# One decoder layer on one core: cached keys worked off inside the attention heads, a filled last head, a new order of the pooling branch, and the samples' projection in 16 matmuls

## What is computed

```python
h = _rms_norm(x, p['g_mix'], RMS_EPS)
z = h @ p['w_in']                      # pool channels u | q | k | v | gate_pool | gate_attn
q = _rope(z[..., OFF_Q:OFF_K]...)
k = _rope(z[..., OFF_K:OFF_V]...)
pool_out = _pool_mixer(u_full, pos, p['w_pool_grp'], p['pool_scale'])
# 4 groups of 128 channels, windows 2, 4, 8, 16: window mean - token, group matmul, scale
# prompt: causal attention; samples: over the cached keys and values and their own
s = jnp.einsum('bqhcd,bkhcd->bhcqk', q, k) * (HEAD_DIM ** -0.5)
p = jax.nn.softmax(s, axis=-1)
a = p[:, :, 0] - lam * p[:, :, 1]
o = jnp.einsum('bhqk,bkhe->bqhe', a, v)
merged = (gate_pool * (pool_out @ p['w_pool_proj'])
          + gate_attn * (o.reshape(B, T, D_ATTN) @ p['w_attn_proj']))
x = x + merged @ p['w_o']
x = x + jnp.square(jax.nn.relu(_rms_norm(x, p['g_mlp'], RMS_EPS) @ p['w_up'])) @ p['w_down']
```

## Time and profile before

| | us |
|---|---|
| median of 3 runs | 1842.93 (1841.47 to 1843.98) |
| the profiled execution | 1843.01 |
| its span | 1841.2 |
| TensorE busy | 1772.3 (96%) |
| VectorE busy | 935.5 (51%) |
| ScalarE busy | 544.3 (30%) |
| GpSimd busy | 244.4 (13%) |

### The profile page before, as it was taken

One profiled execution on the slowest core, in us unless ns is written; L12 is line 12 of the kernel. 1 busy time (PEld: TensorE's weight loads), 2 busy tenths in 40 slices (PEclk: granted clock), 3 DMA queues, 4 the chain that ended last, 5 costly groups with the idle time before them and its releaser, 6 DMA issues.

```text
span 1841.2 us, 27590 instructions
## 1 busy us (share of the span) xinstructions
PE 1772.3 (96%) x11428; PEld 1711.4 (93%) x11428; DVE 935.5 (51%) x1404; ACT 544.3 (30%) x1040; POOL 244.4 (13%) x284
## 2 busy tenths in 40 slices
PE   7999999999969699999999999999999999999997
PEld 6899888988959698999999999999999999999997
DVE  5677777777765987672225434421442244224323
ACT  4355545454543212121113332211220122012202
POOL 3211221222102554520000000000000000000001
PEclk9999999999989898999999999999999999999999
DMA  6211220222024474651122221111111111111112
GB/s 191 59 41 30 70 59 12 70 70 58 13 63 146 135 261 155 217 202 57 46 58 78 74 57 46 46 46 47 46 46 47 46 47 57 47 35 46 58 46 93
DMA packets 177988, 139.03 MB, mean 76 GB/s; under 512 B 7232, under 2 KB 163840, under 8 KB 177855
## 3 DMA queue, kind: packets, MB, share of 16 engines
q1 hardware_dynamic: 176711, 133.07, 23.8%
q10 hardware_dynamic: 1152, 4.19, 0.6%
HBM read 120.29 MB, written 17.18 MB: 75 GB/s over the span
## 4 chain that ended last, share of the span: by engine, by line
PE 82%; DVE 9%; issue 4%; ACT 2%; POOL 1%; DMA 1%; SPq 1%; DVEq 0%; ACTq 0%
PE ps L666 60%; PE ps L580 13%; PE ps L635 3%; PE ps L602 2%; PE ps L625 1%; DVE w_lo L1182 1%; DVE mx L1233 1%; POOL o_rstd L1662 1%; DMA w_raw<-in_w_in 1%; DVE win L1368 1%; DVE y_st L1624 1%; PE ps L799 1%; POOL kv_pages L1684 0%; DVE w_lo L1347 0%; DVE o_st L1268 0%
## 5 line engine op out<-in xcount | busy, mean ns | idle before, releaser
L666 PE MATMUL ps<-h_hi,w_hi 128*128 128x344 f32 x1248 | 270.2, 325 | 7.3 <-DVE w_lo L1347 3.8
L666 PE MATMUL ps<-h_lo,w_hi 128*128 128x344 f32 x1248 | 268.2, 324 | 0.0
L666 PE MATMUL ps<-h_hi,w_lo 128*128 128x344 f32 x1248 | 267.0, 323 | 0.0
L1038 ACT ACTIVATE w_hi<-w_raw 128x1024 fp32r<-128x1024 f32 x106 | 111.9, 1055 | 443.7 <-PE ps L666 439.1
L666 PEld LDWEIGHTS ps<-h_hi,w_hi 128*128 128x128 f32 x1248 | 213.5, 192 | 8.1 <-DVE w_lo L1347 4.1
L666 PEld LDWEIGHTS ps<-h_lo,w_hi 128*128 128x128 f32 x1248 | 214.0, 191 | 0.0
L666 PEld LDWEIGHTS ps<-h_hi,w_lo 128*128 128x128 f32 x1248 | 211.4, 191 | 0.0
L580 PE MATMUL ps<-w_hi,h_hi 128*128 128x384 f32 (+1 forms) x576 | 202.1, 351 | 4.2 <-DVE w_lo L1182 3.7
L580 PE MATMUL ps<-w_hi,h_lo 128*128 128x384 f32 (+1 forms) x576 | 195.7, 340 | 0.0
L580 PE MATMUL ps<-w_lo,h_hi 128*128 128x384 f32 (+1 forms) x576 | 194.9, 338 | 0.0
L1347 DVE TENSOR_TENSOR w_lo<-w_raw,w_hi 128x1024 fp32r<-128x1024 f32 x106 | 138.6, 1308 | 81.5 <-ACT w_hi L1038 81.5
(11 more groups left out here) (221 smaller groups left out, 2782.6 us busy)
## 6 DMA issues: line engine op xcount, KB each, us to landing
w_raw<-in_w_in SPq DMA_DIRECT2D x44, 512.0 KB, 5.5
kv_pages<-in_cache_k SPq DMA_DIRECT2D x32, 512.0 KB, 5.1
kv_pages<-in_cache_v SPq DMA_DIRECT2D x32, 512.0 KB, 5.0
w_raw<-in_w_up SPq DMA_DIRECT2D x32, 512.0 KB, 4.0
w_raw<-in_w_down SPq DMA_DIRECT2D x32, 512.0 KB, 3.6
out<-kv_st SPq DMA_DIRECT2D x16, 512.0 KB
x_in<-in_x_prompt SPq DMA_DIRECT2D x8, 512.0 KB, 5.3
attention_out_scratch<-oT_st ACTq DMA_DIRECT2D x8, 512.0 KB, 2.7
```

The lines of the kernel that those rows point to most:

```text
L666: mm = pe.matmul(ps[:, SET[sp] + c, 0:CH], w, a[:, c * CH:(c + 1) * CH], start=(first and m == 0), stop=(last and m == 2))
L1038: act.activation(w_hi[:, lp], w_raw[:, lp], ACT.Copy).then_inc(s_whi, 1)
```

## The change

1. **Samples' projection.** For heads 1 to 7, tile 8 of `project` uses `h_samples`, written once: columns 0 to 7 the high half of the samples' h, columns 8 to 39 four copies of the low half. One matmul of 40 rows with `w_hi` gives high x high in rows 0 to 7 and low x high in rows 32 to 39, one of 8 rows with `w_lo` the third part: 16 matmuls, not 24. ScalarE copies rows 32 to 39 out (`sample_low`), VectorE adds (`z_smp`), and `rotate` reads `z_smp`.
2. **Keys in the heads.** In head `h`, for each sample `b`, SyncE loads only that head's 128 columns of four pages into a ring of four `key_ring` buffers; GpSimd multiplies all four pages with `q_bc` in one instruction of 128x512 (`key_products`, behind `rotated` of the steps in `KEYS_AT`); VectorE sums them at the end of the step behind (`sum_keys`). `kv_st` shrinks to a ring of four tiles, and SyncE stores each tile for itself (`store_tile`).
3. **Last head.** The product `("u", 0)` is cut into 24 units of three matmuls (one chunk of 344 tokens, one of eight input blocks), spread over the steps of head 7 by `FILL`. ScalarE and VectorE split its weights in steps 0 and 3, not ahead of step 0. The samples' own scores (`own_step`) are in steps 3 to 5.
4. **New order behind.** Two buffers `up`, `u 1`, `u 2` and `u 3` with the group products between them, then gates and pooling projections from tile 7 down to 0; the cached values behind the entries of `VALUES_AFTER`.

```diff
-PART_A = [("u", 0), ("u", 1), ("grp", 0), ("u", 2), ("grp", 1), ("u", 3), ("grp", 2), ("gate", 0), ("grp", 3),
-          ("pool", 0), ("gate", 1), ("pool", 1), ("gate", 2), ("pool", 2),
-          ("gate", 3), ("pool", 3)]
-N_A = 4
-REDUCE_AT = (1, 3, 5, 7, 9, 10, 11, 13)
+PART_A = [("u", 0), ("u", 1), ("u", 2), ("grp", 0), ("u", 3), ("grp", 1), ("gate", 7), ("grp", 2), ("gate", 6), ("grp", 3),
+          ("pool", 7), ("pool", 6)]
+KEYS_AT = {2: (0, 1), 3: (2, 3), 4: (4,), 5: (5,), 6: (6,), 7: (7,)}
...
             def project(hp, t, half):
+                if hp and t == NTT:
+                    for kt in range(4 * half, 4 * half + 4):
+                        both = (bank[0:LOW_ROW + DEC, 0:3 * P], h_smp[:, kt], w_hi[:, :, kt, :])
+                        small = (bank[0:DEC, 0:3 * P], h_smp[:, kt, 0:DEC], w_lo[:, :, kt, :])
...
             def rotate(hp, t):
+                if hp and t == NTT:
+                    dve.wait_ge(s_zl, hp)
+                    dve.tensor_tensor(z_smp[0:n], bank[0:n, 0:3 * P], z_smp[0:n], ALU.add).then_inc(s_zs, 1)
+                    dve.wait_ge(s_zs, hp)
+                    bank = z_smp
...
+            def sum_keys(h, b):
+                dve.wait_ge(s_prod, DEC * h + b + 1)
+                dve.tensor_reduce(sc_all[:, :, b * 16 + 2 * h:b * 16 + 2 * h + 2],
+                                  kc[:, key_slot(h, b)].rearrange("p g (c e) -> p g c e", c=2), AX_X,
+                                  ALU.add).then_inc(s_kred, 1)
...
+                    for b in KEYS_AT.get(s - 1, ()):
+                        sum_keys(h, b)
+                    if not proj and s in (0, 3):
+                        low(s // 3)
+                    if not proj and 3 <= s <= 5:
+                        own_step(s - 3)
...
+            def key_products(h, b):
+                slot = key_slot(h, b)
+                pool.wait_ge(s_qb, 16 * (h + 1))
+                pool.wait_ge(s_kc[slot], 16 * PAGES * (key_uses(h, b) + 1))
+                pool.tensor_tensor(kc[:, slot], kc[:, slot], q_bc[:, b].unsqueeze(1).to_broadcast([P, PAGES, P]),
+                                   ALU.mult).then_inc(s_prod, 1)
...
+            for h in range(HEADS - 1):
+                spread_q(h)
+                for s in range(NTT + 1):
+                    store_tile(h + 1, s)
+                    if s == 1 and h < HEADS - 2:
+                        load_qkv(h + 2)
...
+                    keys_behind(h, s)
...
+            def pool_product(n):
+                if n == KT - 1:
+                    tile_out(pe, grp_tile(NG - 1))
+                product(pool_tile(n), y_hi, y_lo, NG)
```

More of the change, by code:

```diff
@@ L699, in head @@
                         project(h + 1, s, 0)
+                    elif s < NTT:
+                        fill(s, 0)
                     if s == NTT:
@@ L705, in head @@
                         weight_transposes(h, s - 1, 1, proj)
+                    if not proj:
+                        fill(s, 1)
                     if normed and s == 3:
@@ L738, in _, with fill @@
             last = HEADS - 1
-            u_tiles = [t for s_, kind, n, t in part_a() if kind == "u"]
+            filled = [0]
+            def fill(s, place):
+                for unit in range(filled[0], filled[0] + FILL.get((s, place), 0)):
+                    c, kt = unit // KT, unit % KT
+                    if unit == 0:
+                        pe.wait_ge(s_zfree, 9 * HEADS)
+                        pe.wait_ge(s_wlo, W_QKV + 1)
+                    elif kt == 0:
+                        pe.wait_ge(s_u0e, c)
+                    cols_ = slice(c * CH, (c + 1) * CH)
+                    for m, (w, a) in enumerate(((w_hi, h_hi), (w_hi, h_lo), (w_lo, h_hi))):
+                        mm = pe.matmul(bank_z[:, 0:CH], w[:, 0, kt], a[:, kt, cols_], start=(kt == 0 and m == 0),
+                                       stop=(kt == KT - 1 and m == 2))
+                    if kt == KT - 1:
+                        mm.then_inc(s_u0 if c < NCH - 1 else s_tile, 1)
+                filled[0] += FILL.get((s, place), 0)
             def first_product(first, behind):
-                product(u_tiles[0], h_hi, h_lo, KT, part=(first, behind))
+                product(u_tile(1), h_hi, h_lo, KT, part=(first, behind))
             head(last, 1, False, True)
             values(last, 1, NTT - 1)
-            first_product(6, KT)
             def last_head_out():
+                pe.wait_ge(s_us, 1)
                 out_transposes(last, 1, 0, (ps[:, 6], ps[:, 7]))
@@ L823, in _, with group @@
-            pe.wait_ge(s_vout, 2)
-            for i in range(0, DEC // 2):
-                product(gate_tile(i), h_hi, h_lo, KT)
-                cached_values(i, 0)
-                product(pool_tile(i), y_hi, y_lo, NG)
-                cached_values(i, 1)
-            for i in range(DEC // 2, KT - N_A):
-                product(gate_tile(i), h_hi, h_lo, KT)
-                product(pool_tile(i), y_hi, y_lo, NG)
+            def group(g):
+                t = grp_tile(g)
+                pe.wait_ge(s_pllo, g + 1)
+                pe.wait_ge(s_wglo, 1)
+                need(pe, s_free[t[1]], t[0])
+                passes(t[1], wg_hi[:, g], wg_lo[:, g], pl_hi, pl_lo, True, True)
@@ new lines, in gate_product @@
+            def gate_product(n, between=None):
+                product(gate_tile(n), h_hi, h_lo, KT, between=between)
+                if ("gate", n) in VALUES_AFTER:
+                    cached_values(VALUES_AFTER["gate", n])
+            def pool_product(n):
+                if n == KT - 1:
+                    tile_out(pe, grp_tile(NG - 1))
+                product(pool_tile(n), y_hi, y_lo, NG)
+                if ("pool", n) in VALUES_AFTER:
+                    cached_values(VALUES_AFTER["pool", n])
@@ L986, in head @@
                         o_out(h - 1, 1 - par, NTT - 1)
+                    if not proj and s in (3, 6, 8):
+                        first_chunk_out(s // 3 - 1 if s < 8 else 2)
                     if s >= 1:
@@ new lines, in _ @@
+            pooled_high(2)
+            gate_high(7)
+            group_high(2)
+            pooled_high(3)
+            gate_high(6)
+            group_high(3)
+            act.wait_ge(s_tail, NG)
+            act.activation(tail_st[0:BUF + DEC], bank_o[0:BUF + DEC, 0:D_POOL], ACT.Copy).then_inc(s_tailc, 1)
+            next_high(pool_tile(7))
+            next_high(pool_tile(6))
+            for n in range(KT - N_A - 1, -1, -1):
+                gate_high(n)
+                next_high(pool_tile(n))
```

665 lines of the change are left out of this document (365 added, 300 removed).

## The result

The changed kernel takes **1854.75 us** (median of 5 runs, 1851.27 to 1856.55) against 1842.95 for the kernel before in the same session (5 runs, 1841.47 to 1843.98): ratio 1.006, 95% interval 1.0045 to 1.0075. It is 0.6% slower; forecast were 1824 us, with 1800 to 1843 as the range. The profiled execution has a span of 1853.9 us, where before it was 1841.2: 12.7 us more.

What follows compares the result with a forecast made beforehand. It took TensorE as full in middle heads, with VectorE and ScalarE's loop nearly as long, and chains as the bound in the last head; 1843.0 + 12.6 + 3.7 + 9 - 44 = 1824 us, range 1800 to 1843.

Steps and rivals of the forecast that it cites:

- What bounds a middle head: Middle heads: TensorE is full, but VectorE and ScalarE run a loop nearly as long; slack at `bank_z` 1.4 us.
- Rival A: Heads stay TensorE's: slack absorbs the sums and 1.4 us a head are won; 1798 us, chance 0.13.
- The sums up to step 7: Middle heads: VectorE's sums of key products, less a hole they fill, make step 7 run 2.8 us late.
- The tail of a head: From `prob` of step 7 to the next `w_lo`: 6.3 us where it was 7.2; each head 1.8 us longer.
- Head 0: First head: `q_bc` lands at about 92 behind 16 key loads, so VectorE waits for products; +3.7 us once.
- The last head: Last head up to `prob` of step 7: chains of VectorE and ScalarE grow, together +9 us.
- its other terms: Last head, beside sums and hole: `w_lo` splits +2.0, samples' own scores +2.5, chunk copies +0.9, collisions with GpSimd +1.5 us.
- its own gain: Pooling matmuls moved into the last head: 24 units, 11.4 us that leave the stage behind.
- The stage behind: From the last head's `prob` to the first attention gate: 206 us where it was 249.9, so -44.
- Rival B: Stage behind stays half bound by chains, losing 21 us and not 11; 1834, or 1842 with longer heads; chance 0.15.
- Rival C: GpSimd's products meet `ratio`, `prob` or `w_lo` inside heads, up to 1.4 us a collision; 1858 at three a head; chance 0.10.
- +4 a head as the upper end: Heads: upper bound if sums, copy and add count in full (5.8), less the hole (0.71) and 0.8 for the tail.

Runs made afterwards that it cites:

- the two-pass projection alone: The kernel before with only the samples' projection of heads 1 to 7 cut to 16 matmuls, plus copy and add: 1846.32 us, ratio 1.0020.
- the run with one pass: The changed kernel with the samples' projection of heads 1 to 7 back at 24 matmuls, no copy or add: 1847.57 us, ratio 1.0018.
- thin sums: The changed kernel with each sum over cached keys' products taken over 2 of 64 elements, so scores are wrong: 1829.71 us, ratio 0.9925.

## Why the prediction was wrong

The forecast was -18.7 us and the trace shows +12.7; 31 us have to be explained. By its own steps:

1. **What bounds a middle head: right.** VectorE and ScalarE run a loop nearly as long as TensorE's. Rival A (slack absorbs the sums) needed a head of 62.4 us; the two-pass projection alone, without any sum, already takes 64.07.

2. **The sums up to step 7: right in kind, too large.** The forecast had 2.8 us. In a head at full clock `prob` of step 7 starts 56.9 us behind the first `w_lo`, 1.7 later than before. That the head shown above has just 2.8 is the low clock's doing, and chance.

3. **The tail of a head: this step failed.** The forecast let TensorE keep its old times, "0.7 ahead through the shorter first half", held only by the weights of step 7, so that the second half of the projection ends 2.3 us behind them (445.3 against 443.0). But TensorE hadn't kept its times: in the bank that the transposed weights share with q and k it waits for `aT_lo` with each of the tiles 4 to 7, and is as late as VectorE. What stands on TensorE between `aT_lo` of step 6 and the weights of step 7 then counts in full: it comes to these weights 1.74 us after they are there, and its second half ends 4.0 us behind them. The slack had been read at one coupling only, the copy that frees `bank_z` (1.4 us); at the shared bank it was 0.39. From VectorE's add to the next `w_lo` the forecast was right (2.3 us), but the add starts 5.85 us behind the weights and not 4.0. So the tail became 0.9 us longer where 0.9 less was forecast, 1.8 a head. Over six heads that is 11, less 6.6 for the sums that were priced too high, plus 4.3 of low clock: 8.7 of the missing 19.9 - 10.8 = 9.1; the rest is rounding. That the work between counts is shown by the run with one pass (0.7 us more of it, 0.69 later); no run gave q and k a bank of their own. The runs split what heads 1 to 6 lost like this: two-pass projection 0.3 a head (64.07 less 63.75), products, loads and stores 0.1, sums 2.2, which makes 66.37, or 2.6 a head; and 1.07 for the low clock in four of the six: 6 x 2.6 + 4.3 = 19.9. The split hangs on the order: with the sums already there, the two-pass projection costs 0.8 (66.37 less 65.57), and everything else 1.8.

4. **The low clock in the heads: missing from the sum.** The forecast let TensorE wait for the next `w_lo`, and said so, but put no price on the clock behind that wait. It cost 4.3 us, and the copy put first takes it away with the wait.

5. **Head 0: the mechanism was right, the size not.** `q_bc` landed at 94.5 and not at 92, 16 loads took 1.09 us each and not 0.94, and VectorE waited 5.8 us. Of the 9.9 us, 5.0 go with the turned order on SyncE's queue; of the other 4.9, 2.6 are what every head loses at full clock.

6. **The last head: right in sum**, +9.6 for +9, and in part by luck. With the thin sums the last head is 4.5 us shorter, where the forecast had 2.1 for the sums less the hole, so its other terms together were too large. The rows show three of VectorE's `ratio` at 0.7 to 1.3 us, so collisions as forecast (a middle head's eight take 0.23 each; the eight in the last head 0.51 on average), but its own gain was overrated: the fill is worth 6.2 us of span.

7. **The stage behind: the place was right, the size not.** Of the 20.6 us missing there, 4 are work. The other 16.6 are waits and low clock: 5.1 for 3.3 at `pool 7` (3.1 once the page is out of the way, so ScalarE's part was priced right), and 10.6 at two places that the forecast didn't name, each with a stretch at a low clock behind it. The failed sentence is that VectorE's work falls by 56 us "so its chains run ahead". Its sum did fall (194.81 to 133.30 us), but the eight pages of values stayed, their slots go round over four engines, and the order by hand puts them ahead of the low halves. Rival B had this mechanism ("through GpSimd's value products and the order around `pool 7`") and the size of 10 us; measured are 20.6. Spacing the pages alone gave back 10.0, the first page behind `y_lo` 3.5.

8. **Rival C (collisions inside the heads): wrong.** In heads 1 to 6 `ratio` takes 0.225 us (0.221 before) and `prob` of 1024 elements 1.28, as before. The Trainium skill, "GPSIMD Engine Reference", § 1 Specifications, has contention for VectorE instructions with two SBUF inputs. The trace agrees: the sums, with one input, take 0.67 us in the mean of 49 though several ran next to GpSimd's rotations, while the multiply of a page takes 4.0 instead of 2.3.

The range missed too. It took +4 a head as the upper end; +3.3 was measured there, so it held for the heads. It was the sum of two moderate misses on one side, heads and stage behind, which the range treated as alternatives.
